# Hybrid decoder block on one core: six of the eight tiles of the third norm transposed by DMA and VectorE instead of TensorE

## The chip, the cores and the metric

The kernel runs on one core of a Trainium2 chip. The metric is device time in microseconds (us), lower is better, the median of three runs; one further execution was profiled.

## The reference

One layer on x of 1024 tokens by 1024 channels, all float32:

```python
x = x + mix(rmsnorm(x, g_mix)) @ w_out          # conv module and pooling mixer
h = rmsnorm(x, g_ffn)
gu = h @ w_gate_up[i]
x = x + (jax.nn.silu(gu[..., :D_FF]) * gu[..., D_FF:]) @ w_down[i]
gate = jax.nn.sigmoid(rmsnorm(x, g_ple_gate[i]) @ w_ple_gate[i])   # the third norm
e = rmsnorm(p[i] @ w_ple_up[i], g_ple_post[i])
x = x + gate * e
return rmsnorm(x, g_final)
```

The change concerns the third norm, whose result has to reach TensorE with its channels on the partitions, so transposed.

## The kernel before

A tile is 128 tokens by 1024 channels, token on the partition; there are eight. Every float32 factor is split into a high part (rounded to fp32r by ScalarE) and a low part (the rest, by VectorE or GpSimd), and a product is three matmuls, low x high, high x low, high x high: `product`, lines 1604 to 1606. Each large product is done with seven half-size products instead of eight (numbered 1, 2, 6, 5, 7, 3, 4 in the order of `G_ORDER`), for which sums and differences of the quarters of a factor are formed on VectorE.

Each engine works through its own list, written out by hand, in order; semaphores tie them. What a wait holds up is everything behind it on that engine. SyncE (SP) issues almost all DMAs, also in order, and a wait of SP for a store to land holds up the DMAs behind it.

The stage before the change is the down projection: 77 steps (`STEPS`), of which the last eleven are pass 6 (`pi == 6`). A step is 12 matmuls on TensorE (PE), `step_lo` on VectorE (DVE) and `step_hi` on ScalarE (ACT). `step_sum(pi, m)` adds a finished bank to the residual and frees the PSUM bank; `ed_ok` counts them.

Then the gate stage works on four pairs m of tiles, in the order `EVEN_ODD`: tile 2m ("even", tokens' first half of the pair) and tile 2m+1 ("odd"). I write (m, i) for `gate_part(m, i)`: product i of pair m, 12 matmuls. For each tile t:

- `gate_norm(t)` on ACT multiplies the row by its rstd into `xg_place(t)`, two SBUF areas that even and odd tiles take in turn; `xn_ok` counts them.
- `turn(t, 2)` on PE transposes it in eight 128x128 blocks (line 1658) into two PSUM banks: banks 2 and 3 for even tiles, 0 and 1 or 4 and 5 for odd ones; `turned` counts halves of a tile.
- For an even tile `even_high` (ACT) and `even_low` (DVE) make the factors of (m, 1) and (m, 2).
- For an odd tile `a21_copy` and `odd_high` (ACT) read it; `sums(m)` and `last_sum(m)` (DVE, lines 2421 to 2433) combine both tiles, `sum_high` (ACT) and `sum_low` (DVE) split the sums, for (m, 6), (m, 5), (m, 7), (m, 3).

What PE produces is taken up on DVE by `gate_11(m)`, `gate_22(m)`, `gate_12(m)`; (m, 6) and (m, 5) wait for `p1_ok` and `c11_ok` (from `gate_11`), and (m, 4) waits for `c22_ok`, which `gate_22(m)` signals:

```python
                if i == 4:
                    pe.wait_ge(fa_lo, FA + 3 * m + 3)
                    pe.wait_ge(c22_ok, QUADS + m + 1)
```

`gated(t)` and `final(t)` (lines 2465, 2468, 2475) then make the output rows; `final` waits for the rstd of the fourth norm from GpSimd (POOL).

The kernel already has, for four tiles of the second norm, the path that the change uses: `store_xn` (line 600) writes a normed tile to DRAM, `load_xn` (line 606) reads it back in four DMAs whose runs are 32 elements (128 bytes), so that 32x32 blocks change places, and `block_turn` (line 2178) transposes within the blocks by one `dve.transpose` of 128x1024 into SBUF.

Of the kernel before, what the change touches and what calls it, by code (L numbers as in the profile page):

```python
# [31 lines left out]
P = 128  # L32
EPS = 1e-6
BANK = 512
# [5 lines left out]
def hybrid_block(nc, x, p, g_mix, w_in, conv_w, conv_b, ln_g, ln_b, pool_w, pool_scale, w_out,  # L40
# [33 lines left out]
    xn_dram = nc.dram_tensor("xn_scratch", (HT_MIX, P, D), F32, kind="Internal").ap()  # L74
    x1_dram = nc.dram_tensor("x1_scratch", (TT, P, D), F32, kind="Internal").ap()
    in_dram = nc.dram_tensor("in_scratch", (7, PAIRS, P, BANK), F32, kind="Internal").ap()

    with ExitStack() as ctx:
# [79 lines left out]
        def turns(n):  # L158

            return 2 * (n if n < TT + HT_MIX else max(n - HT_MIX, TT))  # L160
# [365 lines left out]
        def _(sp):  # L526
# [172 lines left out]

            def load_e(t):  # L700
                sp.dma_start(e_place(t), e_dram[EVEN_ODD[t]]).then_inc(e_in[t % 3], DMA)
# [8 lines left out]

            sp.wait_ge(ed_mm, 4 * STEPS)
            load_e(0)
            sp.dma_start(raw_b[:, 0, :], g_ple_post[0].partition_broadcast(P)).then_inc(gain_in, DMA)
            load_e(1)
            sp.dma_start(raw_b[:, 1, :], g_final.partition_broadcast(P)).then_inc(gain_in, DMA)
            load_e(2)
# [3 lines left out]
            store_out(1)  # L720
            next_e(5)
# [279 lines left out]
        def _(act):  # L1001
# [355 lines left out]
            def gate_norm(t):  # L1357
                n = 2 * TT + t
                act.wait_ge(rs_ok, n + 1)
                if t >= 2:  # L1360
                    act.wait_ge(turned, turns(n - 1))
                else:
                    act.wait_ge(et_ok, 3 * PAIRS + 2 * (t + 1))
                copy(xg_place(t), x_tile(t, 2).rearrange("p (a n) -> p a n", a=2), xn_ok, scale=rs[:, n:n + 1])

            def even_high(m):
                n = 2 * TT + 2 * m
                for j in range(2):
                    act.wait_ge(turned, turns(n) + j + 1)
# [6 lines left out]
            def a21_copy(m):  # L1376
                act.wait_ge(turned, turns(2 * TT + 2 * m + 1) + 1)
# [4 lines left out]
            def odd_high(m):  # L1382
                act.wait_ge(turned, turns(2 * TT + 2 * m + 1) + 2)
# [108 lines left out]
            for n in range(3, STEPS):  # L1492
# [13 lines left out]
                if n == 6 * PAIRS + 8:  # L1506
                    even_high(0)
# [4 lines left out]

            a21_copy(0)
            odd_high(0)
            sum_high(0, 6)
# [5 lines left out]
            gate_norm(2)  # L1521
            gate_norm(3)
            gate_u2(0)
            sigmoid(0, c11_ok, QUADS + 1)
            even_high(1)
            gate_p5(0)
# [11 lines left out]
            for m in range(1, PAIRS_G - 1):  # L1538
# [6 lines left out]
                gate_norm(2 * m + 2)  # L1545
# [5 lines left out]
                even_high(m + 1)  # L1551
                gate_p5(m)
# [48 lines left out]
        def _(pe):  # L1601
# [30 lines left out]
            def turn(t, norm):  # L1632
                n = norm * TT + t
                for j in range(2):
# [11 lines left out]
                    if norm == 2 and j == 0:  # L1646
                        if t < 2:
                            pe.wait_ge(ed_ok, 24 + 2 * t)
                        elif t % 2 == 0:
                            pe.wait_ge(fs4_ok, FS + t // 2)  # L1650
                            pe.wait_ge(fa_lo, FA + 3 * (t // 2) - 1)
                        elif t == 3:
                            pe.wait_ge(ed_ok, 28)
                        else:
                            pe.wait_ge(fa_lo, FA + 3 * (t // 2))
# [286 lines left out]
            for n in range(STEPS):  # L1942
# [11 lines left out]
                if pi == 6 and j == 6:  # L1954
                    turn(0, 2)
# [31 lines left out]
            turn(1, 2)  # L1987
            pe.wait_ge(pg_lo, len(PG_ORDER))
            for m in range(PAIRS_G):
# [3 lines left out]
                if m + 1 < PAIRS_G:  # L1993
                    turn(2 * m + 2, 2)
                gate_part(m, 5)
                if m + 1 < PAIRS_G:
                    turn(2 * m + 3, 2)
# [6 lines left out]
        def _(dve):  # L2004
# [382 lines left out]

            def even_low(m):
# [8 lines left out]
            for n in range(3, STEPS):  # L2397
# [11 lines left out]
                if n == 6 * PAIRS + 9:  # L2409
                    even_low(0)  # L2410
            for m in range(4):
                step_sum(6, m)

            def sums(m):
                b = odd_bank(m)
                dve.wait_ge(a21_ok, FS - HT_MIX // 2 + m + 1)
                dve.wait_ge(fs34_lo, 2 + 2 * m)
                if m == 0:
# [3 lines left out]
                dve.wait_ge(turned, turns(2 * TT + 2 * m + 1) + 2)  # L2422
# [58 lines left out]
            sum_low(0, 5)  # L2481
            gate_11(0)
            sum_low(0, 7)
            sum_low(0, 3)
            odd_low(0)
            even_low(1)
# [8 lines left out]
            for m in range(1, PAIRS_G - 1):  # L2495
# [3 lines left out]
                odd_low(m)  # L2499
                final(2 * m - 2)  # L2500
# [54 lines left out]
```

## Time and profile before

| what | value |
|---|---|
| median of 3 runs | 1000.47 us (1000.24 to 1000.77) |
| profiled execution, its own time | 1000.92 us |
| span of the profiled execution | 999.0 us |
| busy share PE, DVE, ACT, POOL | 99%, 71%, 46%, 39% |
| granted TensorE clock, mean | 0.997 |
| DMA moved | 142.46 MB, mean 143 GB/s |

An engine's busy share says how long its instructions ran, not whether they set the end; that is read from the chain that ended last, which is followed backwards from the last instruction. Times in the rows are microseconds from the start of the span. Some 1.9 us of the execution's time lie outside the span.

### The profile page before, as it was taken

What the parts mean: (1) busy time and instruction counts of PE and PEld (TensorE: products, weight loads), DVE (VectorE), ACT (ScalarE), POOL (GpSimd) and SP (SyncE); (2) the same over time, 40 slices, a digit from 0 to 9 for tenths busy, and PEclk for the clock granted to TensorE, in tenths of its full rate; (3) what the DMA queues carried; (4) which work ended last, traced back from release to release, by engine and by line L of the source; (5) the groups of instructions that cost most, each with busy time, mean ns of one, the idle gap of its engine ahead of it and who ended that gap; (6) DMA issues with size and microseconds to landing.
All of it is one profiled execution on the core that took longest, in us unless ns stands there. A gap on an engine that the chain in (4) does not pass through costs nothing.

```text
span 999.0 us, 12373 instructions
## 1 busy us (share of the span) xinstructions
PE 987.9 (99%) x4511; PEld 819.0 (82%) x4511; DVE 705.0 (71%) x969; ACT 459.4 (46%) x706; POOL 384.7 (39%) x288
## 2 busy tenths in 40 slices
PE   9999999999999999999999999999999999999996
PEld 7888888888887888888888888888888888888885
DVE  6899999967799355354454444543687888985887
ACT  7625447413363333423333333333445665575775
POOL 3446797711146544444444354351000000011745
PEclk9999999999999999999999999999999999999998
DMA  7421202685525134233333332413998787632222
GB/s 256 141 82 43 82 4 105 212 211 163 153 64 159 53 112 124 81 106 112 99 106 98 114 106 82 130 64 118 366 382 292 239 310 257 195 107 105 85 85 107
DMA packets 120735, 142.46 MB, mean 143 GB/s; under 512 B 22826, under 2 KB 77634, under 8 KB 120674
## 3 DMA queue, kind: packets, MB, share of 16 engines
q1 hardware_dynamic: 120528, 141.40, 43.2%
q8 instruction: 36, 0.59, 0.2%
q10 hardware_dynamic: 146, 0.27, 0.1%
q14 instruction: 25, 0.20, 0.1%
HBM read 106.77 MB, written 34.87 MB: 142 GB/s over the span
## 4 chain that ended last, share of the span: by engine, by line
PE 92%; DVE 3%; issue 2%; ACT 1%; DMA 1%; POOL 1%; SPq 0%; POOLq 0%; ACTq 0%; DVEq 0%
PE ps L1604 30%; PE ps L1606 30%; PE ps L1605 30%; PE ps L1658 1%; DMA raw<-in_w_in 1%; DVE ftmp L2465 0%; ACT junk L1017 0%; DVE resid L2468 0%; DVE spare L2006 0%; PE ps L1762 0%; PE ps L1752 0%; DVE raw_b L2236 0%; DVE raw_b L2230 0%; POOL rs L747 0%; PE ps L1742 0%
## 5 line engine op out<-in xcount | busy, mean ns | idle before, releaser
L744 POOL TENSOR_SCALAR ss<-ss 128x1 f32<-128x1 f32 x38 | 17.7, 467 | 317.1 <-ACT junk L1017 295.8
L2100 DVE SCALAR_TENSOR_TENSOR ps<-resid,convw,ps 128x512 f32<-128x512 f32 x190 | 127.2, 748 | 0.0
L1604 PE MATMUL ps<-ring_hi,ring_lo 128*128 128x512 f32 x308 | 120.0, 390 | 0.1
L1606 PE MATMUL ps<-ring_hi 128*128 128x512 f32 x308 | 119.8, 389 | 0.0
L1605 PE MATMUL ps<-ring_lo,ring_hi 128*128 128x512 f32 x308 | 119.8, 389 | 0.0
L1604 PE MATMUL ps<-act_hi,bs_lo 128*128 128x512 f32 x240 | 93.6, 390 | 0.0
L1606 PE MATMUL ps<-act_hi,bs_hi 128*128 128x512 f32 x240 | 93.4, 389 | 0.0
L1605 PE MATMUL ps<-act_lo,bs_hi 128*128 128x512 f32 x240 | 93.4, 389 | 0.0
L2251 DVE TENSOR_TENSOR gtmp<-ps,gtmp 128x512 f32<-128x512 f32 x22 | 15.2, 691 | 95.5 <-PE ps L1606 95.5
L1003 ACT ACTIVATE ring_hi<-raw 128x512 fp32r<-128x512 f32 x89 | 51.9, 625 | 58.9 <-PE ps L1606 58.8
L750 POOL TENSOR_TENSOR wc_lo<-raw_b,wc_hi 128x1024 fp32r<-128x1024 f32 x22 | 56.1, 2552 | 49.9 <-ACT wc_hi L1003 48.7
L2006 DVE TENSOR_TENSOR ring_lo<-raw,ring_hi 128x512 fp32r<-128x512 f32 x89 | 58.0, 688 | 23.1 <-ACT ring_hi L1003 23.0
L1604 PEld LDWEIGHTS ps<-ring_hi,ring_lo 128*128 128x128 f32 x308 | 57.8, 188 | 12.5 <-DVE ring_lo L2006 0.5
L1606 PEld LDWEIGHTS ps<-ring_hi 128*128 128x128 f32 x308 | 57.8, 188 | 12.1
L1605 PEld LDWEIGHTS ps<-ring_lo,ring_hi 128*128 128x128 f32 x308 | 57.8, 188 | 11.8
L750 POOL TENSOR_TENSOR bs_lo<-raw_b,bs_hi 128x1024 fp32r<-128x1024 f32 x24 | 58.4, 2438 | 20.5 <-ACT bs_hi L1003 12.9
L750 POOL TENSOR_TENSOR bs_lo<-raw,bs_hi 128x1024 fp32r<-128x1024 f32 x17 | 40.7, 2403 | 63.1 <-ACT bs_hi L1003 63.1
L1604 PE MATMUL ps<-act_hi,ws_lo 128*128 128x512 f32 (+1 forms) x144 | 53.5, 371 | 0.5 <-DVE act_lo L2006 0.4
L1604 PEld LDWEIGHTS ps<-act_hi,bs_lo 128*128 128x128 f32 x240 | 45.0, 188 | 9.4
L1606 PEld LDWEIGHTS ps<-act_hi,bs_hi 128*128 128x128 f32 x240 | 45.0, 188 | 9.4
L1606 PE MATMUL ps<-act_hi,ws_hi 128*128 128x512 f32 (+1 forms) x144 | 52.7, 366 | 0.0
L1605 PEld LDWEIGHTS ps<-act_lo,bs_hi 128*128 128x128 f32 x240 | 45.1, 188 | 9.3
(281 smaller groups left out, 2640.7 us busy)
## 6 DMA issues: line engine op xcount, KB each, us to landing
raw<-in_w_gate_up SPq DMA_DIRECT2D x44, 512.0 KB, 5.2
raw<-in_scratch SPq DMA_DIRECT2D x52, 256.0 KB, 3.3
raw<-in_w_down SPq DMA_DIRECT2D x52, 256.0 KB, 4.0
in_scratch<-in_s SPq DMA_DIRECT2D x44, 256.0 KB, 3.3
in_scratch<-gtmp SPq DMA_DIRECT2D x33, 256.0 KB, 2.4
keep<-in_w_down SPq DMA_DIRECT2D x32, 256.0 KB, 4.0
keep<-in_scratch SPq DMA_DIRECT2D x25, 256.0 KB, 3.5
resid<-in_x SPq DMA_DIRECT2D x8, 512.0 KB, 7.1
```

What stands on the lines that cost most here:

```text
L744: pool.tensor_scalar(ss[:, n:n + 1], ss[:, n:n + 1], 1.0 / D, EPS, ALU.mult, ALU.add)\
L750: pool.tensor_tensor(dst, src, hi.bitcast(F32), ALU.subtract).then_inc(done, 1)
L1003: act.activation(dst, src, ACT.Copy, scale=scale).then_inc(done, 1)
L1604: pe.matmul(dst, w_lo_, m_hi, start=start, stop=False, skip_group_check=onto)
L1605: pe.matmul(dst, w_hi_, m_lo, start=False, stop=False, skip_group_check=onto)
L1606: return pe.matmul(dst, w_hi_, m_hi, start=False, stop=stop, skip_group_check=onto)
L1658: ins = pe.transpose(ps[:, turn_bank(norm, t) + j, q * P:(q + 1) * P], xn_cols(n, k), ident[:, :])
L2006: dve.tensor_tensor(dst, src, hi.bitcast(F32), ALU.subtract).then_inc(done, 1)
L2100: dve.scalar_tensor_tensor(out=conv_c if k == last_odd else acc, in0=u_all[:, c, k + h * BANK:k + (h + 1) * BANK], scalar=convw[:, c * 32 ...
L2251: dve.tensor_tensor(gtmp[:, 3, :], ps[:, X_BANK[q % 2], :], gtmp[:, 3, :], ALU.add).then_inc(c22_ok, 1)
```

## The change

Tiles 0, 1, 2, 3, 4 and 6 of the third norm are no longer transposed on PE. ACT writes the normed tile to the same place; SP stores it to DRAM in one DMA (`store_xg`), waits for it to land, and reads it back into the same place in eight DMAs of 64 KB, in runs of 32 elements (`load_xg`); DVE then transposes each half in one instruction of 128x512 into the PSUM banks that PE used to write (`gate_turn`). Tiles 5 and 7 stay on PE. The waits of `turn` on free banks move to `gate_turn`. In the lists: `gate_turn(0)` stands before the last `step_lo`, `gate_turn(1)` after two of the four last `step_sum`, whose other two are put behind `sum_low(0, 5)`; `gate_turn(2)` and `gate_turn(3)` stand together before `even_low(1)`; the others follow `odd_low(m)`. On ACT `even_high(0)` moves behind the last step, and `gate_norm(2)`, `(3)`, `(4)`, `(6)` move to other places. On SP the stores and loads of tiles 0, 1 and 2 come before the first `load_e`, and those of tile 3 after the first two.

```diff
--- before.py
+++ after.py
@@ -72,6 +72,7 @@
...
     xn_dram = nc.dram_tensor("xn_scratch", (HT_MIX, P, D), F32, kind="Internal").ap()
+    xg_dram = nc.dram_tensor("xg_scratch", (TT, 2, P, BANK), F32, kind="Internal").ap()
     x1_dram = nc.dram_tensor("x1_scratch", (TT, P, D), F32, kind="Internal").ap()
@@ -157,7 +158,14 @@
...
-            return 2 * (n if n < TT + HT_MIX else max(n - HT_MIX, TT))
+            by_dve = sum(TT <= k < TT + HT_MIX or 0 <= k - 2 * TT and k - 2 * TT in DVE_TURNS for k in range(n))
+            return 2 * (n - by_dve)
+        DVE_TURNS = (0, 1, 2, 3, 4, 6)
+        def dve_turns(t):
+            return HT_MIX + 2 * DVE_TURNS.index(t)
@@ -697,6 +705,18 @@
...
+            def store_xg(t):
+                sp.wait_ge(xn_ok, 2 * TT + t + 1)
+                sp.dma_start(xg_dram[t].rearrange("h p n -> p h n"), xg_place(t)).then_inc(xn_stored[t % 2], DMA)
+            def load_xg(t):
+                sp.wait_ge(xn_stored[t % 2], DMA * (HT_MIX // 2 + t // 2 + 1))
+                for a in range(P // SQ):
+                    for h in range(2):
+                        src = xg_dram[t, h].rearrange("(b j) (k a i) -> a j k b i", j=SQ, a=P // SQ, i=SQ)[a]
+                        sp.dma_start(xg_place(t)[a * SQ:(a + 1) * SQ, h, :].rearrange("j (k b i) -> j k b i", k=4, i=SQ),
+                                     src).then_inc(xn_in[t % 2], DMA)
             def load_e(t):
@@ -708,16 +728,27 @@
...
+            for t in range(2):
+                store_xg(t)
+                load_xg(t)
+            store_xg(2)
+            load_xg(2)
             sp.wait_ge(ed_mm, 4 * STEPS)
             load_e(0)
+            load_e(1)
+            store_xg(3)
+            load_xg(3)
             sp.dma_start(raw_b[:, 0, :], g_ple_post[0].partition_broadcast(P)).then_inc(gain_in, DMA)
-            load_e(1)
+            load_e(2)
             sp.dma_start(raw_b[:, 1, :], g_final.partition_broadcast(P)).then_inc(gain_in, DMA)
-            load_e(2)
+            store_xg(4)
+            load_xg(4)
             next_e(3)
...
             store_out(1)
+            store_xg(6)
+            load_xg(6)
             next_e(5)
@@ -1357,16 +1388,17 @@
...
                 act.wait_ge(rs_ok, n + 1)
-                if t >= 2:
+                if t == 7:
                     act.wait_ge(turned, turns(n - 1))
+                elif t >= 2:
+                    act.wait_ge(xn_turned, dve_turns(t - 2) + 2)
                 else:
...
             def even_high(m):
-                n = 2 * TT + 2 * m
                 for j in range(2):
-                    act.wait_ge(turned, turns(n) + j + 1)
+                    act.wait_ge(xn_turned, dve_turns(2 * m) + j + 1)
                     if m:
@@ -1374,13 +1406,19 @@
...
             def a21_copy(m):
-                act.wait_ge(turned, turns(2 * TT + 2 * m + 1) + 1)
+                if m < 2:
+                    act.wait_ge(xn_turned, dve_turns(2 * m + 1) + 1)
+                else:
+                    act.wait_ge(turned, turns(2 * TT + 2 * m + 1) + 1)
                 act.wait_ge(fs1_ok, FS + m)
...
             def odd_high(m):
-                act.wait_ge(turned, turns(2 * TT + 2 * m + 1) + 2)
+                if m < 2:
+                    act.wait_ge(xn_turned, dve_turns(2 * m + 1) + 2)
+                else:
+                    act.wait_ge(turned, turns(2 * TT + 2 * m + 1) + 2)
                 if m:
@@ -1503,26 +1541,26 @@
...
                     gate_norm(n - 6 * PAIRS - 5)
-                if n == 6 * PAIRS + 8:
-                    even_high(0)
...
+            even_high(0)
+            gate_norm(2)
             a21_copy(0)
             odd_high(0)
+            gate_norm(3)
             sum_high(0, 6)
...
             square_odd(4)
-            gate_norm(2)
-            gate_norm(3)
             gate_u2(0)
...
             even_high(1)
+            gate_norm(4)
             gate_p5(0)
@@ -1542,13 +1580,14 @@
...
                     square_odd(7)
-                gate_norm(2 * m + 2)
                 square_out(2 * m - 2)
...
                 even_high(m + 1)
+                if m == 1:
+                    gate_norm(6)
                 gate_p5(m)
@@ -1644,15 +1683,7 @@
...
                     if norm == 2 and j == 0:
-                        if t < 2:
-                            pe.wait_ge(ed_ok, 24 + 2 * t)
-                        elif t % 2 == 0:
-                            pe.wait_ge(fs4_ok, FS + t // 2)
-                            pe.wait_ge(fa_lo, FA + 3 * (t // 2) - 1)
-                        elif t == 3:
-                            pe.wait_ge(ed_ok, 28)
-                        else:
-                            pe.wait_ge(fa_lo, FA + 3 * (t // 2))
+                        pe.wait_ge(fa_lo, FA + 3 * (t // 2))
                     for q in range(4):
@@ -1951,8 +1982,6 @@
...
                     step_mm(n, m).then_inc(ed_mm, 1)
-                if pi == 6 and j == 6:
-                    turn(0, 2)
@@ -1984,16 +2013,13 @@
...
-            turn(1, 2)
             pe.wait_ge(pg_lo, len(PG_ORDER))
...
                 gate_part(m, 6)
-                if m + 1 < PAIRS_G:
-                    turn(2 * m + 2, 2)
                 gate_part(m, 5)
-                if m + 1 < PAIRS_G:
+                if m in (1, 2):
                     turn(2 * m + 3, 2)
@@ -2385,6 +2411,17 @@
...
+            def gate_turn(t):
+                dve.wait_ge(xn_in[t % 2], DMA * (P // SQ) * (HT_MIX // 2 + 2 * (t // 2 + 1)))
+                if t in (0, 1, 3):
+                    dve.wait_ge(ed_ok, {0: 24, 1: 26, 3: 28}[t])
+                else:
+                    dve.wait_ge(fs4_ok, FS + t // 2)
+                    dve.wait_ge(fa_lo, FA + 3 * (t // 2) - 1)
+                bank = 2 if t % 2 == 0 else odd_bank(t // 2)
+                for j in range(2):
+                    dve.transpose(ps[:, bank + j, :], xg_place(t)[:, j, :]).then_inc(xn_turned, 1)
             def even_low(m):
@@ -2407,19 +2444,25 @@
...
                 if n == 6 * PAIRS + 9:
-                    even_low(0)
-            for m in range(4):
-                step_sum(6, m)
+                    gate_turn(0)
+            even_low(0)
+            step_sum(6, 0)
+            step_sum(6, 1)
+            gate_turn(1)
...
                 dve.wait_ge(fs34_lo, 2 + 2 * m)
+                dve.wait_ge(xn_turned, dve_turns(2 * m) + 2)
                 if m == 0:
...
                 dve.tensor_tensor(x_sum(7), quarter(2), g_a21, ALU.subtract).then_inc(fs3_ok, 1)
-                dve.wait_ge(turned, turns(2 * TT + 2 * m + 1) + 2)
+                if m < 2:
+                    dve.wait_ge(xn_turned, dve_turns(2 * m + 1) + 2)
+                else:
+                    dve.wait_ge(turned, turns(2 * TT + 2 * m + 1) + 2)
                 if m == 0:
@@ -2479,10 +2522,14 @@
...
             sum_low(0, 5)
+            step_sum(6, 2)
+            step_sum(6, 3)
             gate_11(0)
...
             odd_low(0)
+            gate_turn(2)
+            gate_turn(3)
             even_low(1)
@@ -2497,6 +2544,7 @@
...
                 odd_low(m)
+                gate_turn(2 * m + 2)
                 final(2 * m - 2)
```

## Rows read from the trace of the kernel before

**Rows 1.** Page, the chain that ended last, by engine.
```profile
PE 92%; DVE 3%; issue 2%; ACT 1%; DMA 1%; POOL 1%; SPq 0%; POOLq 0%; ACTq 0%; DVEq 0%
```

**Rows 2.** The chain in order of time: start us, us, what.
```profile
907.94 0.87 PE ps L1658 x8
908.82 0.23 PE ps L1604
...
917.00 0.87 PE ps L1658 x8
...
935.17 0.47 PE ps L1604
...
958.88 0.25 PE ps L1606
```

**Rows 3.** Timeline of DVE in the gate stage: start us, us, instruction, [idle before].
```profile
905.99 2.73 DVE L2386 TENSOR_TENSOR resid<-resid,ps 128x512 f32<-128x512 f32 x4 [4.05 <-issue]
...
911.75 0.69 DVE L2006 TENSOR_TENSOR spare<-ftmp,spare 128x512 fp32r<-128x512 f32 x1
...
918.67 1.29 DVE L2006 TENSOR_TENSOR spare<-ps,spare 128x512 fp32r<-128x512 f32 x2 [1.80 <-ACT spare L1003]
922.84 0.69 DVE L2421 TENSOR_TENSOR raw<-ps,scr 128x512 f32<-128x512 f32 x1 [2.87 <-ACT scr L1003]
...
924.76 0.68 DVE L2453 TENSOR_TENSOR ftmp<-ps,ftmp 128x512 f32<-128x512 f32 x1
...
935.25 0.69 DVE L2448 TENSOR_TENSOR ftmp<-ps,ftmp 128x512 f32<-128x512 f32 x1 [0.93 <-PE ps L1606]
...
942.78 1.28 DVE L2475 SCALAR_TENSOR_TENSOR resid<-resid,rs,raw_b 128x1024 f32<-128x1024 f32 x1 [0.72 <-POOL rs L747]
...
947.10 0.68 DVE L2453 TENSOR_TENSOR ftmp<-ps,ftmp 128x512 f32<-128x512 f32 x1
```

**Rows 4.** Timeline of SP's DMA issues, second norm, tiles 2 and 3.
```profile
235.38 0.32 SPq L600 DMA_DIRECT2D xn_scratch<-scr  x1
238.71 3.34 SPq L606 DMA_DIRECT2D scr<-xn_scratch  x4
242.09 0.67 SPq L600 DMA_DIRECT2D xn_scratch<-scr  x1
245.93 3.01 SPq L606 DMA_DIRECT2D scr<-xn_scratch  x4
```

**Rows 5.** Timeline of DVE, second norm, transposes of tiles 2 and 3.
```profile
245.07 1.25 DVE L2178 STREAM_TRANSPOSE raw<-scr 128x1024 f32<-128x1024 f32 x1 [4.28 <-DMA scr<-xn_scratch]
...
251.73 1.25 DVE L2178 STREAM_TRANSPOSE raw<-scr 128x1024 f32<-128x1024 f32 x1 [2.22 <-DMA scr<-xn_scratch]
```

**Rows 6.** Line 606's DMA issues: ns min/median/max, first and last start.
```profile
L606 SPq DMA_DIRECT2D scr<-xn_scratch x16: 563/688/1274, 215.0 to 248.0; - x16
```

**Rows 7.** Line 582, stores of 512 KB: time to landing.
```profile
DMA to landing us min/median/max: 2.6/2.6/6.9
```

**Rows 8.** Timeline of ACT: `gate_norm(0)`.
```profile
887.97 1.14 ACT L1003 ACTIVATE keep<-resid,rs 128x1024 f32<-128x1024 f32 x1
```

**Rows 9.** Timeline of SP's DMA issues about the gate stage's start.
```profile
884.99 0.43 SPq L656 DMA_DIRECT2D keep<-in_w_down  x1
907.97 0.33 SPq L701 DMA_DIRECT2D raw<-e_scratch  x1
```

**Rows 10.** Windows: stretch, us, busy PE, PEld, DVE, ACT, POOL, granted clock, DMA share, GB/s.
```profile
912.00:914.00 2.00, 2.00 (x11) 1.65 (x10) 1.14 (x2) 2.00 (x5) 0.00 (x0) 1.00 0.89 287
991.00:993.00 2.00, 0.00 (x0) 0.00 (x0) 1.79 (x5) 1.78 (x6) 0.54 (x1) 1.00 0.01 4
993.00:994.00 1.00, 0.00 (x0) 0.00 (x0) 0.54 (x2) 0.74 (x3) 0.94 (x2) 0.92 0.00 0
```

**Rows 11.** Timeline of PE at the kernel's start.
```profile
1.66 2.50 PE L1665 MATMUL ps<-ident 128*128 128x128 f32 x10 [1.66 <-POOL ident L765]
...
7.36 1.08 PE L1665 MATMUL ps<-ident 128*128 128x128 f32 x8
```

## The prediction

> **What bounds the kernel now.** I read the chain that ended last first: 92% of it is PE [rows 1], so time taken off PE counts unless another engine takes over. Next came the chain in order of time through the gate stage, to see where PE leads. A tile's transposes stand on it as 0.87 us, and three parts fill 908.82 to 917.00, so a part (m, i) is 2.73 us [rows 2]. The chain leaves PE for good after (2, 6), at 959.1 [rows 2]; from there DVE, with POOL's and ACT's norms, sets the end, and PE time saved behind that point brings nothing. Then DVE's timeline, for what stands between a turned tile and the part that needs it [rows 3]; the path through DRAM where the kernel already has it [rows 4 to 7]; and SP's own list, to see when it is free [rows 9]: its last issue of the down projection ends at 885.4 and the next starts at 907.97.
>
> **What is removed.** Six tiles times 0.87 us = 5.2 us of PE. Tiles 0 to 3 (3.5 us) are turned while PE leads. Tile 4 lies in m = 1, where DVE takes 12.5 us from `gate_11(1)` at 935.25 to the end of `gate_22(1)`, 947.10 + 0.68 [rows 3], while PE needs, from 935.17 on, four parts and two tiles' transposes, about 12.9 us (4 x 2.73 + 1.74 = 12.7, plus some 0.2 that it runs slower there). Without one of them PE would be at (1, 4) after 12.1 us and wait for DVE: 0.4 us of the 0.87 is kept. Tile 6 is turned behind 959.1 and brings nothing. So with nothing late the gain is 3.5 + 0.4 = 3.9 us, not 5.2.
>
> **What is added on DVE.** Twelve transposes of 128x512. The nearest row is 1.25 us for 128x1024 into SBUF [rows 5]; half of it is 0.63 us, and the ceiling I take is that writing PSUM costs twice that, 1.25. I take 0.63, since reading PSUM costs DVE's other instructions of 128x512 nothing beyond 0.69 [rows 3]. Tiles 0 to 2 find DVE idle (it waited 4.05 us before 905.99, and 1.80 and 2.87 us in the next 17 us). Tiles 4 and 6 stand before `final`, where DVE waits for POOL's rstd: 0.72 us before 942.78 [rows 3], and the `final` ahead of it waits for its own. I take their 1.25 us to disappear in the two waits; with the ceiling price, 1.2 us each would not. Only tile 3's 1.3 us stand on the path below.
>
> **What is added on SP.** Per tile: the store (S), the eight issues of the load, which wait for it (I), and the landing after the last issue (L). S: in the second norm 3.33 us (235.38 to 238.71) and 3.84 [rows 4]; 2.6 us for a lone store [rows 7]. The queue is empty here, so I take 2.8, between 2.6 and 3.8. I: four issues of 128 KB took 3.0 and 3.3 us [rows 4], each 0.56 to 0.69 with the queue free [rows 6]. Now there are eight of half the size. If only the bytes count, 3.0 us; if each issue costs what a full one did, 8 x 0.69 = 5.5. I take 4.1 (some 0.5 us each): the lone issue of 0.56 us has a part that doesn't halve. L: from 242.05 to 245.07 and from 248.94 to 251.73 [rows 4, 5], 3.0 and 2.8; the last piece is smaller, so 2.8, bounds 2.5 and 3.0.
>
> SP stands idle from 885.4, and `gate_norm(0)` ends at 887.97 + 1.14 = 889.1 [rows 8, 9]. One tile holds SP for S + I = 6.9 us, and tiles follow one another:
> - tile 0: loads issued by 896.0, landed 898.8
> - tile 1: 902.9, landed 905.7
> - tile 2 (its norm is ready at about 902.7, after `gate_turn(0)` and `even_high(0)`): 909.8, landed 912.6
> - `load_e(0)` and `load_e(1)`: 0.8 us, 910.6
> - tile 3: its store now queues behind 1 MB of those loads. At 287 GB/s, which such loads reach [rows 10], that is 3.6 us, and at the 340 I estimate for the bare transfer 3.0. So it has landed at 910.6 + 2.8 + 3.0 = 916.4, loads are issued by 920.5, landed 923.3.
>
> **Who waits for them.** PE would start (0, 1) at 908.82 - 1.74 = 907.08. Tile 0 is needed by then through `even_low(0)`, which can end at about 903.5: on time. Tile 1: `sum_low(0, 6)` ends 4.0 us after `a21_copy(0)`, at 911.75 + 0.69 for a transpose that began at 907.94 [rows 2, 3]. `gate_turn(1)` can start at 906.5, after two step sums, whatever the landing at 905.7, so that chain ends near 911 and (0, 6) comes at 907.08 + 5.45 = 912.5: on time. Tile 2 isn't wanted before DVE is through with `odd_low(0)`, 916.
>
> Tile 3 is the late one. `gate_turn(3)` stands before `even_low(1)`, `sums(1)` and `gate_22(0)` in DVE's list, and DVE reaches it at 917.3. All of these wait, and (0, 4) waits for `gate_22(0)`. After the landing: 0.1 for the signal, 1.3 two transposes, 1.2 `even_low(1)` (918.67, two at 0.6), and 2.6 from 922.84 to the end of `gate_22(0)`, 924.76 + 0.68 [rows 3]: 5.2 us. PE is ready for (0, 4) at 907.08 + 6 x 2.73 = 923.4; before, it began it at 926.97 (917.00 + 2 x 0.87 + 3 x 2.73 = 926.9). So PE waits from a landing at 918.2 on, and the end moves by (landing + 5.2) - 926.97 - 0.4 = landing - 922.2. With 923.3: PE idle for 5.1 us and the end 1.1 us later.
>
> **The clock.** After PE's last product, at 991.0, the granted clock was whole until 993 and 0.92 in the microsecond behind it, so it fell to the lower level at 993.8, after 2.8 us of idle PE [rows 10]. At the start, ten small matmuls take 2.50 us from 1.66 on and eight of the same take 1.08 from 7.36 on [rows 11]: PE worked up to 5.7 us at the lower level (1.2 GHz) before it had the upper one (2.4 GHz). An idle PE of 5.1 us thus likely loses the clock, and the parts after it run at half speed for up to 5.7 us, a loss of 0 to 2.9 us; I take 2.0. PE leads there until `gate_11(1)`, so it counts whole.
>
> The Trainium skill (page "TensorE: Matmul & The Clock Gate", Part 1) says that an idle TensorE drops to 1.2 GHz and comes back after sustained work; by it alone the fall would be the rule for a gap of this length, and the trace agrees, with 2.8 us at the end.
>
> **Sum.** 1000.92 (the profiled execution; span 999.0 and 1.9 around it) - 3.9 + 5.0 (1.1 + 3.9, the lateness of tile 3) + 2.0 = 1004.0. The runs' median lies 0.45 below the profiled one: 1003.6 us.
>
> **Rivals.**
> 1. Not late enough to matter, on the faster side. What decides is when tile 3 lands. With S 2.6, I 3.0, L 2.5 and a queue wait of 2.0, tile 2 starts at 902.7, and its loads are out by 908.3; tile 3's store goes at 909.5, when `gate_norm(3)` is done, and it lands at 919.6. PE waits 1.4 us, keeps its clock, and the end moves by -2.6: 997.9. If the landing were at 918.2 or earlier, -3.9: 996.6. For it: the 3.0 us for a whole tile [rows 4]. Against it: three serial tiles must all keep the lowest price. It is faster by over 0.2% (2 us) for landings before 920.2.
> 2. Even. Landings from 920.2 to about 922.5 give -2.0 to +0.3, and with part of the clock's price up to +2: 998.5 to 1002.5.
> 3. Eight issues at 0.69 each (I 5.5), S 3.8, L 3.0: tile 2's loads are out at 917.0, tile 3 lands at 933.1. The end moves by 10.9 + 2.9: 1014. For it: nothing shows that a smaller issue is cheaper [rows 6]. With S at 2.8 it is about 1009.
> 4. Runs of 128 bytes are slow as such. Moving 512 KB so took 3.0 to 3.3 us of issues and 2.8 more in the second norm [rows 4, 5], which is in the sum; it would need another rate for the same pattern.
>
> The Trainium skill (page "VectorE: DVE Perf Modes", section "The three transpose paths") warns that a plain DMA copy that transposes by strides is 19 times slower than the hardware transpose. Taken on the estimate of 340 GB/s that is 29 us per tile; with four tiles in series, tile 3 would land near 1020 and the kernel end near 1098 us. The rows speak against it here: 6 us from the first load's issue to the turn.
>
> **Chances.** Forecast, slower by 2 to 8 us: 0.50. Far slower (rival 3): 0.11. Even: 0.26. Faster (rival 1): 0.12. Rival 4 at another rate: 0.01. So faster by over 0.2% 0.12, within 0.2%, which is about what can be told from no change, 0.26, slower 0.62. Range: 998.5 leaves out rival 1, 1009 the worse part of rival 3, together about 0.2. The forecast's own range is 1002.5 to 1008.
>
> **What would show it.** `gate_turn(3)` on DVE preceded by several us of idle time released by the DMA of the scratch tensor, a gap on PE before (0, 4), the granted clock below 1 about 930, PE's eight-block groups gone but for two in the gate stage, and twelve transposes of 0.63 us. Wrong would be: issues under 0.45 us each, a store of tile 3 not held up by `load_e`, or a PE gap elsewhere, above all before (0, 1) or (0, 6).

## The result, and the profile after

The kernel with the change takes 1012.38 us (median, 1012.05 to 1012.95) against 1000.36 us beside it on the same chip: 1.0124 times as long, interval 1.0112 to 1.0136. It is slower, as forecast, but by 12.0 us where 3.1 was forecast, and outside the range. The profiled execution took 1012.57 us (span 1010.5).

The page of the changed kernel, chain that ended last, by engine (before: [rows 1]):

```profile
PE 87%; DVE 3%; SPq 2%; DMA 2%; issue 2%; ACT 2%; POOL 1%; POOLq 0%; ACTq 0%; DVEq 0%
```

PE has given up 5 points, and SP's queue and DMA, which were at 0 and 1%, hold 2% each. Where that is, SP's own list says (timeline of SP, start and duration in us; before: [rows 9]):

```profile
883.77 0.43 SPq L664 DMA_DIRECT2D keep<-in_w_down  x1
887.91 0.38 SPq L710 DMA_DIRECT2D xg_scratch<-keep  x1
890.71 5.32 SPq L717 DMA_DIRECT2D keep<-xg_scratch  x8
896.07 0.63 SPq L710 DMA_DIRECT2D xg_scratch<-keep  x1
899.37 5.54 SPq L717 DMA_DIRECT2D keep<-xg_scratch  x8
904.96 0.62 SPq L710 DMA_DIRECT2D xg_scratch<-keep  x1
908.09 5.31 SPq L717 DMA_DIRECT2D keep<-xg_scratch  x8
913.44 1.10 SPq L721 DMA_DIRECT2D raw<-e_scratch  x2
914.58 0.43 SPq L710 DMA_DIRECT2D xg_scratch<-keep  x1
920.90 5.32 SPq L717 DMA_DIRECT2D keep<-xg_scratch  x8
926.26 0.63 SPq L741 DMA_DIRECT2D raw_b<-in_g_ple_post  x1
926.93 0.43 SPq L721 DMA_DIRECT2D raw<-e_scratch  x1
927.40 0.43 SPq L743 DMA_DIRECT2D raw_b<-in_g_final  x1
```

This trace runs about 1.2 us ahead of the one before when the stage begins (883.77 against 884.99 [rows 9]), so 1.2 us are to be added wherever times of the two are set against each other. A tile holds SP for 8.1 to 8.8 us: the store until it has landed (2.80, 3.30, 3.13) and eight issues (5.3 to 5.5). Tile 3's store goes out behind the 1 MB of `load_e` and takes 6.32 us. And, not foreseen, the load of `g_final` stands behind all of it and is issued at 927.40.

One line's DMA issues, ns min/median/max (before: [rows 6]):

```profile
L717 SPq DMA_DIRECT2D keep<-xg_scratch x48: 557/637/644, 890.7 to 963.8; - x48
```

An issue of 64 KB costs 637 ns where one of 128 KB cost 688: for half the bytes nearly the same.

Timeline of DVE, the end of each row is what ended the idle time before it (before: [rows 3]):

```profile
898.10 1.32 DVE L2423 STREAM_TRANSPOSE ps<-keep 128x512 f32<-128x512 f32 x2 [1.13 <-DMA keep<-xg_scratch]
...
906.87 1.32 DVE L2423 STREAM_TRANSPOSE ps<-keep 128x512 f32<-128x512 f32 x2 [1.65 <-DMA keep<-xg_scratch]
...
927.99 1.32 DVE L2423 STREAM_TRANSPOSE ps<-keep 128x512 f32<-128x512 f32 x2 [10.45 <-DMA keep<-xg_scratch]
...
932.31 0.68 DVE L2496 TENSOR_TENSOR ftmp<-ps,ftmp 128x512 f32<-128x512 f32 x1
...
934.21 3.37 DVE L2032 TENSOR_TENSOR spare<-ftmp,spare 128x512 fp32r<-128x512 f32 x2 [0.62 <-ACT spare L1034]
...
938.10 3.40 DVE L2032 TENSOR_TENSOR spare<-raw,spare 128x512 fp32r<-128x512 f32 x2
...
942.74 1.23 DVE L2511 TENSOR_TENSOR resid<-resid,ftmp 128x1024 f32<-128x1024 f32 x1
```

DVE stands for 10.45 us before `gate_turn(3)`. From the start of that turn to the end of `gate_22(0)` (932.31 + 0.68) it is 5.0 us. Then two pairs of low parts take 3.4 us each. Before, the first pair took 3.37 us too, and the second 1.30 (timeline of DVE before):

```profile
926.67 3.37 DVE L2006 TENSOR_TENSOR spare<-ftmp,spare 128x512 fp32r<-128x512 f32 x2 [0.62 <-ACT spare L1003]
...
930.56 1.30 DVE L2006 TENSOR_TENSOR spare<-raw,spare 128x512 fp32r<-128x512 f32 x2
```

Timeline of PE, the first products behind its gaps:

```profile
933.14 0.77 PE L1643 MATMUL ps<-t_scr,a_form 128*128 128x512 f32 x1 [10.07 <-DVE ftmp L2496]
933.71 0.63 PE L1644 MATMUL ps<-t_scr,a_form 128*128 128x512 f32 x1
...
936.13 0.40 PE L1644 MATMUL ps<-t_gain,a_form 128*128 128x512 f32 x1
...
944.82 0.47 PE L1643 MATMUL ps<-bs_hi,spare 128*128 128x512 f32 x1 [1.95 <-ACT ftmp L1034]
```

There are two large gaps: 10.07 us before (0, 4), the forecast place, and 1.95 us before (1, 6), which was not forecast. The second leads back from PE to ACT's copy into `ftmp`, from there to `gated(0)` on DVE, and from there to POOL and its gains (timelines of ACT and of POOL):

```profile
944.08 0.60 ACT L1034 ACTIVATE ftmp<-ps 128x512 f32<-128x512 f32 x1 [3.23 <-DVE resid L2511]
```

```profile
934.04 2.39 POOL L985 TENSOR_TENSOR raw<-raw,raw_b 128x1024 f32<-128x1024 f32 x1 [12.39 <-DMA raw_b<-in_g_final]
```

POOL waited 12.39 us for `g_final`, and its two products (934.04 and 937.96) then ran beside both pairs of DVE's low parts. Before, the two products started at 923.19 and 926.48, and only the second of them met a pair of low parts, the first one.

Windows (us; busy time and instructions of PE, PEld, DVE, ACT, POOL; granted clock, DMA share, GB/s):

```profile
920.00:925.00 5.00, 3.07 (x14) 2.22 (x12) 0.00 (x0) 0.74 (x2) 0.74 (x2) 1.00 0.36 62
925.00:930.00 5.00, 0.00 (x0) 0.00 (x0) 2.01 (x4) 1.25 (x2) 0.00 (x0) 0.57 0.79 167
930.00:935.00 5.00, 1.86 (x5) 1.50 (x6) 4.35 (x7) 3.50 (x8) 0.96 (x1) 0.50 0.88 307
...
945.00:950.00 5.00, 5.00 (x16) 3.92 (x16) 4.96 (x4) 2.72 (x6) 4.83 (x4) 0.66 0.18 41
```

The clock fell to 1.2 GHz at about 925.7, some 2.6 us after PE stopped, and was back about 935.9. The first seven products after the gap take 2.99 us (933.14 to 936.13); at 0.23 us each, and 0.1 more for the first, it would be 1.7: 1.3 us lost. It fell once more at about 946.2, after the 1.95 us gap and with PE already at work, for some 3.5 us: 1.6 us lost.

Summed up, as far as (2, 6), behind which the chain leaves PE: five tiles no longer turned there -4.4; waits before (0, 6) 0.54, (0, 4) 10.07, (1, 6) 1.95, (1, 4) 0.36; clock 1.3 and 1.6. Behind (2, 6), DVE's turn of tile 6 adds 0.6 (shown below). That is 12.0. The span grew by 11.5, and with the 1.2 us that this trace ran ahead by 12.7; the medians grew by 12.0. The 0.7 us between 12.0 and the traces' 12.7 isn't assigned to anything.

### The profile page after: what moved, and what is told of

Its sections match the earlier page's. It is cut to its first block, busy times and chain, and to the rows that moved or that the text cites. A ratio compares the mean times of both kernels' runs of the same rounds, so it can differ in the third digit from the quotient of the medians.

```text
span 1010.5 us, 12343 instructions
## 1 busy us (share of the span) xinstructions
PE 986.1 (98%) x4463; PEld 815.9 (81%) x4463; DVE 713.0 (71%) x981; ACT 460.0 (46%) x706; POOL 384.8 (38%) x288
## 4 chain that ended last, share of the span: by engine, by line
PE 87%; DVE 3%; SPq 2%; DMA 2%; issue 2%; ACT 2%; POOL 1%; POOLq 0%; ACTq 0%; DVEq 0%
PE ps L1643 28%; PE ps L1645 28%; PE ps L1644 28%; SPq L717 2%; DMA xg_scratch<-keep 2%; DVE spare L2032 1%; PE ps L1689 1%; DMA raw_b<-in_g_final 1%; DVE ftmp L2508 1%; ACT junk L1048 1%; DVE resid L2511 0%; ACT act_hi L1034 0%; PE ps L1783 0%; PE ps L1793 0%; PE ps L1696 0%
## 5 line engine op out<-in xcount | busy, mean ns | idle before, releaser
L1644 PE MATMUL ps<-act_lo,ws_hi 128*128 128x512 f32 (+1 forms) x144 | 52.6, 366 | 0.0
```

The lines of the kernel that those rows point to most:

```text
L1644: pe.matmul(dst, w_hi_, m_lo, start=False, stop=False, skip_group_check=onto)
```

## Experiments

**No way through DRAM.** Is "nothing late" worth 3.9 us? All stores and loads of the six tiles go, and DVE transposes the tiles straight from `keep`; the 32x32 blocks then stay in their places, so the gate is computed from channels in another order, and only SP's list is shorter:

```diff
-            for t in range(2):
-                store_xg(t)
-                load_xg(t)
...
             def gate_turn(t):
-                dve.wait_ge(xn_in[t % 2], ...)
+                dve.wait_ge(xn_ok, 2 * TT + t + 1)
```

> The changed kernel without the way through DRAM: no store and no load of the six tiles, so that VectorE transposes the blocks in place and the blocks don't change places (the gate is computed from wrongly ordered channels). PE, ACT and DVE do the same work in the same order. Theory A (the lateness of the transfers is the whole loss): nothing is late, the gate stage gains what four PE transposes in front and 0.4 us in pair 1 give, 3.9 us: 996.6 us. Rival B (the twelve DVE transposes and the rearranged lists cost time by themselves): 1000 us or more, with gaps on PE though nothing waits for a DMA.

Measured: 998.7 us, 0.9983 (0.9973 to 0.9992) of before; 1.4 us gained, not 3.9. Everything beyond that, 13.7 us, is the way through DRAM and what it delays. No DMA is late, and yet PE has gaps of 0.35, 1.11 and 0.78 us ahead of (2, 6). The timelines of PE and of DVE:

```profile
922.90 0.47 PE L1632 MATMUL ps<-t_scr,a_form 128*128 128x512 f32 x1 [0.35 <-DVE ftmp L2485]
...
932.47 0.47 PE L1632 MATMUL ps<-bs_hi,spare 128*128 128x512 f32 x1 [1.11 <-ACT ftmp L1023]
```

```profile
923.97 3.36 DVE L2021 TENSOR_TENSOR spare<-ftmp,spare 128x512 fp32r<-128x512 f32 x2 [0.62 <-ACT spare L1023]
```

Part (1, 6) can't start before `gated(0)` is through on DVE: `gate_p1(1)` waits for it, and (1, 6) for `gate_p1(1)`. Before, that chain and PE came out together. So PE time saved ahead of (1, 6) is only kept as far as DVE follows.

And tile 6's turn isn't free. The timelines of DVE, before and in this version, between `odd_low(2)` and `even_low(3)`:

```profile
962.77 1.28 DVE L2475 SCALAR_TENSOR_TENSOR resid<-resid,rs,raw_b 128x1024 f32<-128x1024 f32 x1 [1.29 <-POOL rs L747]
```

```profile
957.56 1.31 DVE L2412 STREAM_TRANSPOSE ps<-keep 128x512 f32<-128x512 f32 x2
...
960.74 1.28 DVE L2507 SCALAR_TENSOR_TENSOR resid<-resid,rs,raw_b 128x1024 f32<-128x1024 f32 x1 [0.71 <-POOL rs L767]
```

DVE's wait for POOL's rstd shrinks only from 1.29 to 0.71 us for 1.2 us of transposes, and from the start of `odd_low(2)` to that of `even_low(3)` it is 4.98 us instead of 4.37, in the changed kernel as in this version. These 0.6 us lie on the chain that ends last. Together: 3.9 - 1.11 - 0.35 - 0.31 (0.78 less the 0.47 that was forecast) - 0.6 = 1.5 us, against 1.4 by the medians.

**DVE's order.** `even_low(1)` and `gate_22(0)` don't read tile 3; they move ahead of its turn:

```diff
             gate_turn(2)
-            gate_turn(3)
             even_low(1)
-            sums(1)
             gate_22(0)
+            gate_turn(3)
+            sums(1)
```

> The changed kernel with only the order on DVE altered: even_low(1) and gate_22(0), which need nothing of tile 3, stand before gate_turn(3). Theory A (two causes: tile 3 lands late, and g_final lands late so that POOL's products for gated(0) come late): the gap before (0, 4) goes, but (1, 6) still waits for gated(0), which waits for POOL's first product at about 936.5; (1, 6) starts at about 941 instead of 944.8: 1008 us. Rival C (tile 3's landing is the only cause): (1, 6) starts when its sums are ready, about 934: 1001 to 1003 us.

Measured: 1012.53 us, 1.0120 (1.0105 to 1.0136), as slow as the change itself. The gap before (0, 4) is gone, and a single one of 12.11 us stands before (1, 6) (timelines of PE and of POOL):

```profile
944.29 0.76 PE L1643 MATMUL ps<-bs_hi,spare 128*128 128x512 f32 x1 [12.11 <-ACT ftmp L1034]
```

```profile
935.46 2.35 POOL L985 TENSOR_TENSOR raw<-raw,raw_b 128x1024 f32<-128x1024 f32 x1 [12.88 <-DMA raw_b<-in_g_final]
```

The queue behind `gate_turn(3)` is thus where the stall shows, not why the kernel is late: (1, 6) starts at 944.29 instead of 944.82, 1.4 us earlier if the 0.9 us by which this trace started later is taken out, and behind the one long gap the lower clock costs 2.7 us. Expected were 1008 us and a start near 941; what that left out is what POOL's two products do to DVE's operations with both operands in SBUF, a low pair and the last sum of `gated(0)`, 3.25 us each where they take 1.3 and 1.2 without (timeline of DVE):

```profile
935.71 3.25 DVE L2032 TENSOR_TENSOR spare<-raw,spare 128x512 fp32r<-128x512 f32 x2
...
940.18 3.25 DVE L2511 TENSOR_TENSOR resid<-resid,ftmp 128x1024 f32<-128x1024 f32 x1
```

**The gains ahead of tile 3's loads**, in SP's order:

```diff
             store_xg(3)
-            load_xg(3)
             sp.dma_start(raw_b[:, 0, :], g_ple_post...)
-            load_e(2)
             sp.dma_start(raw_b[:, 1, :], g_final...)
+            load_xg(3)
+            load_e(2)
```

> The changed kernel with only SP's order altered: the two gains g_ple_post and g_final are loaded between the store and the loads of tile 3, not after its loads. Theory A (their late landing makes the second gap on PE, 1.95 us before (1, 6), and with it the second stretch at the lower clock, about 1.5 us): both go, the gap before (0, 4) stays at 10 us or grows by up to 1: 1009 us. Rival C (tile 3's landing is the only cause, the second gap is an after-effect of DVE's backlog): 1012 us, second gap still there.

Measured: 1010.67 us, 1.0103 (1.0088 to 1.0118). The gap before (1, 6) is gone, as expected of it, POOL's product comes at 924.40; but 1 MB more stands ahead of tile 3, which is turned 1.8 us later (930.54 instead of 927.99, less the 0.7 us by which this trace started later). Its issues are hardly later, it lands 3.3 us after the last of them instead of 1.8 (timelines of DVE and of PE):

```profile
930.54 1.32 DVE L2423 STREAM_TRANSPOSE ps<-keep 128x512 f32<-128x512 f32 x2 [12.25 <-DMA keep<-xg_scratch]
```

```profile
935.69 0.77 PE L1643 MATMUL ps<-t_scr,a_form 128*128 128x512 f32 x1 [11.86 <-DVE ftmp L2496]
```

**Both of these together.**

> Both orders together: even_low(1) and gate_22(0) before gate_turn(3) on DVE, and the two gains before tile 3's loads on SP. Theory A, as it now stands: each alone changed little because the other cause then led. With both, (1, 6) waits for gate_p1(1), this for gated(0), and this on DVE for tile 3 through sums(1) and its low parts: tile 3 lands at about 930.5, gated(0) ends near 939.7, (1, 6) starts near 940.5 instead of 944.8: 1004.5 us. Rival D (nothing but the sums stands between tile 3 and (1, 6)): (1, 6) at 935, 1001 us. If the two causes aren't the ones: no change, 1010 to 1012 us.

Measured: 1009.04 us, 1.0092 (1.0077 to 1.0107). Part (1, 6) starts at 941.26, 0.8 us from the place expected. That is 3.5 us before the changed kernel's 944.82, which would make 1008.9; the expected time was wrongly carried over from the place. One large gap of 9.82 us is left, and DVE waits 8.03 us for tile 3. What is left is tile 3 itself, which is late.

**Sixteen issues a tile instead of eight**, half the size each:

```diff
                     for h in range(2):
...
+                        for c in range(2):
+                            r = slice(c * SQ // 2, (c + 1) * SQ // 2)
...
+                            dst = xg_place(t)[a * SQ:(a + 1) * SQ, h, :][r]
```

> The changed kernel with each tile's load in sixteen issues of 32 KB instead of eight of 64 KB, same bytes, same runs of 128 bytes. If an issue costs SP about 0.67 us whatever its size: 10.6 us per tile instead of 5.3, tile 3 lands 20 us or more later, over 1030 us. If the cost is that of the bytes or the runs: 5.3 us per tile, 1012 us.

Measured: 1033.37 us, 1.0327 (1.0312 to 1.0343). Line 720's issues, and the timeline of SP for tile 1:

```profile
L720 SPq DMA_DIRECT2D keep<-xg_scratch x96: 557/612/1187, 891.0 to 989.4; - x96
```

```profile
905.24 10.39 SPq L720 DMA_DIRECT2D keep<-xg_scratch x16
```

688 ns for 128 KB [rows 6], 637 for 64, 612 for 32, each the median: the cost of an issue hardly depends on its size. With twice the issues every tile is late, and PE has gaps of 3.15, 5.68, 0.93 and 16.28 us.

**Tile 3 back on PE, the other five as in the change** (the waits on tile 3 move back with it).

```diff
-        DVE_TURNS = (0, 1, 2, 3, 4, 6)
+        DVE_TURNS = (0, 1, 2, 4, 6)
...
-            store_xg(3)
-            load_xg(3)
```

> The changed kernel with tile 3 turned on PE again, so five tiles by DMA and DVE and no store or load of tile 3; the loads behind it on SP come earlier by some 12 us. Theory A (the lateness of tile 3 and of what stands behind it on SP is the loss; tiles 0, 1, 2, 4 and 6 are on time): about what the version without DRAM gives, 998.8 us. Rival E (the way through DRAM costs also where it is on time, by its traffic or its place on SP): over 1001 us.

Measured: 1003.26 us, 1.0039 (1.0024 to 1.0054). Some 9 us are back, but not the 13.6 expected: SP is busy with tile 2 until 913.36, `g_final` is issued at 915.49, POOL's first product starts at 924.28, and PE waits 2.73 us before (1, 6). So the gains are late without tile 3 too.

**Tile 3's store ahead of `load_e`**, with the two orders above:

```diff
             sp.wait_ge(ed_mm, 4 * STEPS)
-            load_e(0)
-            load_e(1)
             store_xg(3)
-            load_xg(3)
+            load_e(0)
             ... g_ple_post, g_final ...
+            load_xg(3)
+            load_e(1)
```

> All six tiles by DMA and DVE, even_low(1) and gate_22(0) before gate_turn(3), and SP's order: store of tile 3, load_e(0), both gains, loads of tile 3, load_e(1), load_e(2). Theory A (tile 3's store lay 3 us behind 1 MB of loads): it lands at 917.5 instead of 921, tile 3 near 924.5, gated(0) ends near 934, (1, 6) starts near 934.7: 999.5 to 1000.5 us. If the wait for the store was not that of the queue but of the store: as the fifth experiment.

Measured: 1008.05 us, 1.0082 (1.0066 to 1.0099). The timeline of SP:

```profile
913.99 0.57 SPq L710 DMA_DIRECT2D xg_scratch<-keep  x1
...
917.46 7.49 SPq L717 DMA_DIRECT2D keep<-xg_scratch  x8
```

The store lands in 3.47 us instead of 6.32, so the megabyte ahead of it did cost 2.9 us. But now the eight loads stand behind 1.5 MB, and their issues take 7.49 us instead of 5.3. The wait has moved from the store to the loads; tile 3 is turned at 926.75, and 8.28 us of idle PE are left before (1, 6). The expectation, 1000 us, was missed by 8: tile 3 came 2.2 us later than it said, and from the turn to the end of `gated(0)` it is 12.4 us (926.75 to 939.18) instead of 9.5, 1.9 of them a wait for ACT.

**The clock.** First, in the version with the gains early, products on `ident` whose result nothing reads keep PE busy through its gap:

```diff
                 gate_part(m, 3)
+                if m == 0:
+                    keep_warm(90)
                 gate_part(m, 4)
```

> The third experiment (gains early, otherwise the changed kernel) with 90 small matmuls put on PE between (0, 3) and (0, 4), into a bank that is free, about 10 us, to fill the gap of 11.9 us. If the lower clock behind the gap counts (12 products and more at 0.43 us instead of 0.23 from 935.7 to 941): granted clock 1 throughout, 2 to 2.6 us less than the third experiment, 1008.3 us. If DVE leads there anyway and the clock costs nothing: 1010.7 us.

Measured: 1016.93 us, 1.0173 (1.0158 to 1.0189). The 90 took 20.26 us, 8 us more than the gap, so this says nothing on the clock. With 50 of them, 11.3 us:

> The sixth experiment again with 50 small matmuls in place of 90: each is two matmuls of 0.11 us, so 90 took 20 us and overfilled the gap; 50 take 11.1 us against a gap of 11.9 in the third experiment. If the lower clock behind the gap counts: granted clock 1 throughout and 2 to 2.6 us less than the third experiment (1010.7): 1008.3 us. If it costs nothing because DVE leads: 1010.7 us.

Measured: 1009.1 us, 1.0089 (1.0075 to 1.0103), against 1.0103 (1.0088 to 1.0118) without them: the intervals overlap, so the times alone don't decide. The windows, and the timeline of DVE at `gate_11(1)`, once of this run and once of the one without the fifty:

```profile
925.00:930.00 5.00, 5.00 (x48) 5.00 (x47) 0.67 (x2) 0.00 (x0) 1.21 (x1) 1.00 0.61 109
930.00:935.00 5.00, 5.00 (x44) 4.91 (x43) 4.90 (x9) 3.41 (x7) 3.07 (x3) 1.00 0.56 178
```

```profile
943.03 0.69 DVE L2493 TENSOR_TENSOR ftmp<-ps,ftmp 128x512 f32<-128x512 f32 x1 [1.80 <-PE ps L1645]
```

```profile
946.76 0.69 DVE L2491 TENSOR_TENSOR ftmp<-ps,ftmp 128x512 f32<-128x512 f32 x1 [4.33 <-PE ps L1645]
```

With PE busy the clock stays whole, and from the start of (0, 4) to `gate_11(1)` it is 8.5 us (934.49 to 943.03) instead of 11.1 (935.69 to 946.76). The fallen clock so costs 2.5 us in this stretch, as expected; from (0, 4) to the last part, (3, 4), 2.0 of them are left (61.8 us instead of 63.8). It is the small part: 9 us are lost without it.

**The late gain alone**: the version without the way through DRAM, but with `g_final` loaded about where the change has it:

```diff
             load_e(2)
+            sp.wait_ge(pg_mm, 8)
             sp.dma_start(raw_b[:, 1, :], g_final...)
```

> The version without the way through DRAM (998.7 us), with nothing changed but that SP issues g_final's load only after (1, 1) is done, near 926, so that it lands near 931 instead of about 914. No tile is late here. Theory A (the late gain has a cost of its own, through POOL's products, gated(0) and gate_p1(1) to (1, 6)): PE waits about 6 us before (1, 6), with a stretch at the lower clock behind it: 1005 us. Rival C (only tile 3's landing counts): 998.7 us.

Measured: 1009.11 us, 1.0090 (1.0076 to 1.0104). Expected were 1005. Against the same version with the gain on time it is 10.4 us slower, and no tile is late (timelines of POOL and of PE):

```profile
932.13 2.34 POOL L975 TENSOR_TENSOR raw<-raw,raw_b 128x1024 f32<-128x1024 f32 x1 [12.06 <-DMA raw_b<-in_g_final]
```

```profile
937.96 0.77 PE L1633 MATMUL ps<-bs_hi,spare 128*128 128x512 f32 x1 [7.06 <-ACT ftmp L1024]
```

PE waits 7.06 us before (1, 6), loses the clock (fourteen products at 0.43 us, 2.8 us), and waits 2.19 us more behind it. So two things are late, each of which costs about 10 us by itself: the gain 10.4, tile 3 with the gains early 12.0 against the same version, 1.8 of them for its own later turn. They lie side by side in time, which is why the gains early gave only 1.7 us and DVE's order nothing.

**Five tiles, and the gains ahead of tile 2's loads.** If the two causes are all, this should be faster than before.

```diff
             store_xg(2)
-            load_xg(2)
             load_e(0)
+            ... g_ple_post, load_e(1), g_final ...
+            load_xg(2)
```

> The seventh experiment (tile 3 on PE, 1003.3 us) with SP's order altered: load_e(0), the gains and load_e(1) before tile 2's loads, as soon as the down projection's last product is done, at about 907 instead of 914. Theory A (its loss against the version without DRAM, 4.6 us, is the gains' lateness: POOL's products start 3.8 us later, run beside DVE's low parts and lengthen them, and (1, 6) waits 2.7 us): 999 us. Rival E (the transfers cost by their traffic): 1003 us.

Measured: 1003.55 us, 1.0035 (1.0022 to 1.0047). The timeline of SP:

```profile
908.93 8.18 SPq L717 DMA_DIRECT2D keep<-xg_scratch  x8
```

Behind 2 MB the eight issues take 8.18 us, tile 2 is turned at 919.09 instead of 916.24, and now it is tile 2 that pushes ACT, POOL and DVE back (gaps of 1.33, 1.18 and 1.09 us). In neither of the two orders tried does one queue bring three tiles and the gains in time. The time is the one that rival E named, so it doesn't decide against it, but the traces leave it little. The last part starts 4.2 us later than in the version without DRAM (the traces' starts taken out), and of these the turn of tile 3 on PE is 0.9, the longer waits 2.1 and the wait before (0, 6) 0.44. That leaves 0.7 us for restarts and for the traffic of the transfers together.

**Two tiles only.** Tiles 0 and 1 are stored and loaded while SP has nothing else to do; the others stay on PE, and the rest of SP's order is that of before:

```diff
-        DVE_TURNS = (0, 1, 2, 3, 4, 6)
+        DVE_TURNS = (0, 1)
```

> Only tiles 0 and 1 by DMA and DVE, the other six on PE as before; SP is through with both at 905, before it could issue load_e(0) in any case. Theory A (what is on time and stands in no one's way gains its PE time, less what tile 1 is late): 1.74 us less, and 0.6 us for the wait of (0, 6) that all runs with this path show: 1.1 us faster than before, 999.0 to 999.4 us, ratio 0.9989. Rival E: no gain, ratio 1.000 or more.

Measured: 999.22 us (11 runs) beside 999.89: 0.9991 (0.9982 to 1.0000). That is the expected place, the best version that goes through DRAM, and at the edge of what can be told from no change. The timeline of PE has one gap:

```profile
912.43 0.50 PE L1635 MATMUL ps<-bs_hi,spare 128*128 128x512 f32 x1 [0.68 <-DVE spare L2032]
```

## Why the prediction was right in direction and wrong in size

The path was right (tile 3 late, DVE behind it, (0, 4), the clock). Three steps failed: the price of a load's issues, the gain with nothing late, and what stands behind tile 3 in SP's queue, which has no term at all.

- **The issues of a load (I), the term that was mis-sized most.** Taken: 4.1 us for eight; measured: 5.32, 5.54, 5.31, 5.32. Over the four tiles ahead of (0, 4) that is 5.1 us. The prediction had the row that says so, 688 ns an issue [rows 6], and chose the middle between "bytes" and "issues" because of one issue of 563 ns. Sixteen issues of half the size (1033.37 us) settle it.
- **Store and landing.** S 2.8, measured 2.80, 3.30, 3.13; the store behind `load_e` 5.8, measured 6.32 (the 340 GB/s behind its 3.0 us of waiting stand in no row); L 2.8, measured 1.8 for tile 3. Together with 0.3 us more for `load_e`, some 0.7 more. So tile 3 landed at 927.9 where 923.3 was forecast, 5.8 us later with the 1.2 us between the traces.
- **Who waits for tile 3.** Right: `gate_turn(3)`, then 5.2 us from the landing to the end of `gate_22(0)` (measured 5.1), then (0, 4). PE's wait was 10.07 us instead of 5.1. The order of DVE's list, which makes (0, 4) wait, turned out to be without weight for the time (1012.53 us without it).
- **"With nothing late the gain is 3.9 us."** Wrong: 1.4 us. The prediction looked at DVE's lead over PE for tile 4 and overlooked that (1, 6) hangs on `gated(0)`, through `gate_p1(1)`, and that this chain was already level with PE. 1.11 us come back there, 0.35 before (0, 4), 0.78 instead of 0.47 before (1, 4), and 0.6 at the turn of tile 6.
- **What stands behind the moved work in SP's queue.** The step that is missing altogether. The prediction costed `load_e` ahead of tile 3, and not the gains behind it. Its own schedule had tile 3's loads issued by 920.5, so `g_final` out at about 921.6 (an estimate, with the 1.1 us between the two in the trace); with tile 3 on PE it went out at 917.0 in the same count of time, and PE waited 2.73 us already. POOL gets `g_final` at 934.0, its products then meet DVE's low parts, `gated(0)` is late, and (1, 6) waits 1.95 us more; with no tile late, a gain as late as that costs 10.4 us. Behind the wait came a second fall of the clock (1.6 us).
- **The clock.** Right in kind: 2.0 taken for one fall, 1.3 measured for it, and 2.9 for the two that came.
- **`gate_turn(1)`** was forecast to be on time for (0, 6); PE waited 0.54 us (0.68 with two tiles). Its loads' issues took 5.54 us, so it landed about 906.8, and without the way through DRAM there is no such wait.
- **DVE's transposes** into PSUM: 0.63 us each taken, 1.31 to 1.32 us a pair measured. Right. That tiles 4 and 6 disappear in waits was wrong for tile 6, by 0.6 us.
- **The rivals.** The third came closest, by the right mechanism: no smaller issue is cheaper. With S at 2.8 it was put at about 1009, and the gain's lateness and the second clock drop (1.95 and 1.6) are about what it lacks to 1012.4. That its 1014 lies near is partly luck: it took S at 3.8 and L at 3.0, where 2.8 to 3.3 and 1.8 were measured, and had no term for the gains. The stride rule of the Trainium skill (page "VectorE: DVE Perf Modes", section "The three transpose paths") did not show here: tiles 0, 1 and 3 took 7.1 to 7.5 us from the first issue to the turn, 5.3 to 5.5 of them issues, against the 29 us of that estimate. The page states the rule for a large stride of the innermost dimension at the destination, a condition that the prediction left out; here 32 elements lie together on both sides.

Open: whether four issues a tile, both halves in one, would bring tile 3 in time was not tried, nor was a second queue for the gains. Why issues right behind 1.5 to 2 MB of loads take longer is not shown either, only that they do.

## To carry to other kernels

Count DMA issues, not bytes, when a queue has to wait for a store and then issue a load in pieces; and when work moves into a queue, follow what stands behind it to its last reader, as carefully as the work itself. Time saved on the engine that leads is kept only as far as the next engine in the chain has slack: find the row where the two are level before pricing the gain. Two causes that lie side by side hide each other: that removing one brings nothing does not clear it, and it takes a run with that one alone to see its price.

## What the runs showed of the hardware

- A DMA issue on SP takes 0.61 to 0.69 us (medians) at 32, 64 and 128 KB, in 32-element runs; issued within about 1 us of 1.5 to 2 MB of other loads it takes 0.94 to 1.02 on the mean (7.49 and 8.18 us for eight).
- A store of 512 KB in this stage landed after 2.80 to 3.47 us with no large load right ahead of it, and after 6.32 behind 1 MB of loads.
- A pair of DVE's low parts with both operands in SBUF took 3.25 to 3.40 us where it met a product of 128x1024 on POOL (2.12 where it met only the end of one), and 1.29 alone; the sums that read PSUM stayed at 0.68 beside POOL's product at 923.19 before. The Trainium skill (page "SBUF — State Buffer", section "SBUF: two separate sides") says that an operation of VectorE with two SBUF inputs and one of GpSimd that reads SBUF shut each other out of a shared port for a whole instruction; the trace agrees.
- The granted clock fell 2.6, 3.6 and 4.3 us after PE stopped (the change, gains early, DVE's order), and was back after 2.8, 5.3 and 5.9 us of work. Shorter gaps can cost it too, with PE at work again when it falls: those of 1.95 us (the change), 2.73 (tile 3 on PE) and 3.15 (sixteen issues) did, those of 2.19 (the late gain alone) and 1.33 (five tiles, gains ahead) did not.
